# Delta rule: step sizes as logarithms in the decays' exponents, and the decay columns of all tiles from one PSUM bank

## The reference, cut to what matters

```
q = l2norm(q) * DK**-0.5;  k = l2norm(k)
beta = sigmoid(gb);  g = -exp(A_log) * softplus(ga + dt_bias)
gc = cumsum(g);  decay = exp(gc_t - gc_s)            (t >= s)
L  = beta_t * (k k^T) * decay                         (t > s);   A = L + I
u, w = A^-1 [ v * beta | k * (beta * exp(gc)) ]
v_new = u - w S;   qk = (q k^T) * decay
o = (q * exp(gc)) S + qk v_new
S_new = S * exp(g_last) + (k * exp(g_last - gc))^T v_new
```

## Time and profile before

| | |
|---|---|
| time, median of 3 runs | 945.67 us (945.03 to 946.57) |
| span of the profiled execution, first to last instruction | 943.7 us |
| the profiled execution's own time | not listed apart; the median stands 1.97 us above the span |
| PE / weight load / DVE / ACT / POOL busy | 99% / 89% / 69% / 48% / 18% |
| tile loop, 220.87 to 255.01 us | 34.14 us: PE 34.14, DVE 26.96, ACT 22.81, POOL 19.30 busy |
| elimination, 255.01 to 283.38 us | 28.37 us: PE 27.68, DVE 21.46, ACT 20.11, POOL 18.29 busy |

### The profile page before, as it was taken

The page is one execution under the profiler, slowest core; times in us unless marked ns, Lnnn a source line. Parts: engine busy times, 40 slices in busy tenths (PEclk is TensorE's granted clock), DMA queues, the critical chain, the costliest instruction groups (busy, mean ns, idle before and its releaser), DMA issues.

```text
span 943.7 us, 16891 instructions
## 1 busy us (share of the span) xinstructions
PE 931.8 (99%) x6919; PEld 841.9 (89%) x6919; DVE 648.3 (69%) x1083; ACT 452.1 (48%) x836; POOL 170.0 (18%) x198
## 2 busy tenths in 40 slices
PE   9999999999999999999999999999999999999998
PEld 7899888998889877799888999999999999888886
DVE  7627888777775565552666999999999999435321
ACT  6634454648566454554654445444444445333310
POOL 0071101103664331000002032222222220000000
PEclk9999999999999999999999999999999999999999
DMA  8624142121104084244904322222222224412221
GB/s 303 225 88 145 54 168 93 47 94 49 45 5 135 2 290 154 82 142 157 317 18 138 113 87 90 90 90 90 88 73 74 79 89 152 147 64 93 78 89 56
DMA packets 73820, 103.70 MB, mean 110 GB/s; under 512 B 2576, under 2 KB 53904, under 8 KB 73360
## 3 DMA queue, kind: packets, MB, share of 16 engines
q1 hardware_dynamic: 73744, 102.63, 32.6%
HBM read 92.27 MB, written 10.35 MB: 109 GB/s over the span
## 4 chain that ended last, share of the span: by engine, by line
PE 51%; DVE 3%; ACT 2%; POOL 1%; issue 1%; ACTq 0%; POOLq 0%; DVEq 0%
PE bank L1222 8%; PE bank L1220 8%; PE bank L1221 8%; PE bank L538 5%; PE bank L537 5%; PE bank L536 5%; PE bank L484 2%; PE bank L486 1%; PE bank L485 1%; PE bank L466 1%; PE bank L562 1%; PE bank L1034 1%; PE bank L564 1%; PE bank L563 1%; PE bank L1036 1%
## 5 line engine op out<-in xcount | busy, mean ns | idle before, releaser
L2168 DVE TENSOR_TENSOR wlo<-wraw,whi 128x2048 fp32r<-128x2048 f32 (+1 forms) x56 | 126.2, 2253 | 102.2 <-ACT whi L1617 93.0
L1617 ACT ACTIVATE whi<-wraw 128x2048 fp32r<-128x2048 f32 (+1 forms) x58 | 109.3, 1885 | 101.9 <-PE bank L538 72.8
L498 PE MATMUL bank<-hhi,whi 128*128 128x320 f32 x352 | 116.4, 331 | 0.6 <-issue 0.6
L500 PE MATMUL bank<-hhi,wlo 128*128 128x320 f32 x352 | 108.7, 309 | 0.0
L499 PE MATMUL bank<-hlo,whi 128*128 128x320 f32 x352 | 108.7, 309 | 0.0
L498 PEld LDWEIGHTS bank<-hhi,whi 128*128 128x128 f32 x352 | 66.2, 188 | 5.0 <-issue 3.6
L499 PEld LDWEIGHTS bank<-hlo,whi 128*128 128x128 f32 x352 | 66.2, 188 | 3.0 <-issue 2.4
L500 PEld LDWEIGHTS bank<-hhi,wlo 128*128 128x128 f32 x352 | 66.1, 188 | 0.0
L536 PE MATMUL bank<-whi,hhi 128*128 128x512 f32 x150 | 58.4, 389 | 0.0
L537 PE MATMUL bank<-wlo,hhi 128*128 128x512 f32 x150 | 58.4, 389 | 0.0
L538 PE MATMUL bank<-whi,hlo 128*128 128x512 f32 x150 | 58.3, 389 | 0.0
(11 more groups left out here) (491 smaller groups left out, 2690.4 us busy)
## 6 DMA issues: line engine op xcount, KB each, us to landing
wraw<-in_w_in SPq DMA_DIRECT2D x13, 1024.0 KB, 5.5
wraw<-in_w_gate SPq DMA_DIRECT2D x11, 1024.0 KB, 5.2
wraw<-in_w_up SPq DMA_DIRECT2D x11, 1024.0 KB, 5.1
wraw<-in_w_down SPq DMA_DIRECT2D x10, 1024.0 KB, 5.1
kTs<-in_cache_sb_k SPq DMA_DIRECT2D x8, 512.0 KB, 4.4
vraw<-in_cache_sb_v SPq DMA_DIRECT2D x8, 512.0 KB, 4.9
wraw<-in_w_mix_out SPq DMA_DIRECT2D x4, 1024.0 KB, 6.3
kmT<-in_cache_mem_k SPq DMA_DIRECT2D x8, 512.0 KB, 6.2
```

What stands on the lines that cost most here:

```text
L498: T.matmul(o, wh[:, k, cs], hhi[:, k, hs], start=(k == 0), stop=False)
L500: ins = T.matmul(o, wl[:, k, cs], hhi[:, k, hs], start=False, stop=(k == KD - 1))
L1617: V(wv(whi, i), wv(wraw, i), ACT.Copy).then_inc(s["w_hi_ready"], 1)
L2168: V.tensor_tensor(wv(wlo, i), wv(wraw, i), wv(whi, i).bitcast(F32), ALU.subtract)\
```

## The change

The step size enters as a logarithm. With softplus(-gb) = -log(beta), one absolute value, exponential and logarithm on 40 columns serve both gates (`gsoft`). `lnc` is the log norm of the key minus softplus(-gb) minus `vscale`, and it is subtracted from the summed g in column form, so the exponentials already hold beta and the norms' ratio; the values are scaled by `vscale` in place of `beta`. Gone are `ratio`, `beta`, POOL's `beta_source`, PE's `beta_rows`, DVE's second product on `LT` and its product on `bege`. The clamp RMAX is 60 in place of 14. The columns of all tiles are made at once, by five matmuls into one bank, in front of the first "grow". ACT takes their exponentials once, after tile 1's large ones.

```diff
-RMAX = 14.0
+RMAX = 60.0
-        rsrc = [[at(f"rsrc{n}{m}", [P, HEADS, P], CQ + TILE * (2 * n + m)) for m in range(2)] for n in range(2)]
+        rsrc = [at(f"rsrc{n}", [P, HEADS, P], CQ + TILE * n) for n in range(2)]
...
@@ block.tensor @@
+            def decay_columns():
+                b = take(("gcol", 0))
+                of_tiles = gdec[:, 0:PT, :].rearrange("p t h -> p (t h)")
+                T.matmul(gcol(b, "sum"), uptri[:, :], of_tiles, start=True, stop=True)
+                T.matmul(gcol(b, "all"), ones[:, :], of_tiles, start=True, stop=True)
+                T.matmul(gcol(b, "own"), ones[:, :], flat(gown), start=True, stop=True)
+                T.matmul(gcol(b, "sum16"), up16[:, :], gdec[:, PT, :], start=True, stop=True)
+                done(T.matmul(gcol(b, "all16"), same16[:, :], gdec[:, PT, :], start=True, stop=True), ("gcol", 0))
             def decay_rows(i):
-                b = take(("gcol", i))
-                T.matmul(bank[b][:, 0:4], (uptri if i < PT else up16)[:, :], gdec[:, i, :], start=True, stop=True)
-                if i == PT:
-                    T.matmul(bank[b][:, 8:8 + HEADS * DEC_BATCH], ones[:, :], flat(gown), start=True, stop=True)
-                done(T.matmul(bank[b][:, 4:8], (ones if i < PT else same16)[:, :], gdec[:, i, :],
-                              start=True, stop=True), ("gcol", i))
                 pe.wait_ge(s["decay_src"], i + 1)
...
-            def beta_rows(i):
-                pe.wait_ge(s["beta_src"], i + 1)
-                b = take(("brow", i))
-                done(T.matmul(bank[b][:, :], ones[:, :], flat(rsrc[i % 2][1]), start=True, stop=True), ("brow", i))
...
             pe.wait_ge(s["gates"], 1)
+            decay_columns()
             decay_rows(0)
             for i in range(NT):
...
-                beta_rows(i)
@@ block.gpsimd @@
-            def beta_source(i):
...
-                G.tensor_tensor(rsrc[i % 2][1][:, :, :], spread(ident[:, :], 1, [P, HEADS, P]),
-                                spread(ratio[:, i, :], 2, [P, HEADS, P]), ALU.mult).then_inc(s["beta_src"], 1)
@@ block.scalar @@
             for i in range(NT):
-                evacuated(e, ("gcol", i))
-                V(kdec[:, i, :], gcs[:, i, 2, :], ACT.Exp)
-                V(bege[:, i, :], gcs[:, i, 3, :], ACT.Exp)
...
                 e.wait_ge(s["dif_ready"], i + 1)
                 V(scr[4 + i % 2][:, :, :], scr[4 + i % 2][:, :, :], ACT.Exp).then_inc(s["dt_ready"], 1)
...
                 V(scr[6 + i % 2][:, :, :], quad(b), ACT.Exp).then_inc(bank_free[b], 1)
+                if i == 1:
+                    V(kdec[:, :, :], gcs[:, :, 2, :], ACT.Exp)
+                    V(bege[:, :, :], gcs[:, :, 3, :], ACT.Exp)
+                    V(etot[:, 0:PT, :], gcs[:, 0:PT, 1, :], ACT.Exp)
+                    V(etotS[:, :, :], etotS[:, :, :], ACT.Exp).then_inc(s["small_exp"], 1)
@@ block.vector @@
             def log_norms():
-                link(V.tensor_tensor(ratio[:, :, :], lnr[:, :, :, 1], lnr[:, :, :, 0], ALU.subtract))
...
+                link(V.tensor_tensor(vscale[:, :, :], lnr[:, :, :, 0], lnr[:, :, :, 1], ALU.subtract))
+                link(V.tensor_tensor(lnc[:, :, :], lnr[:, :, :, 1], gsoft[:, 1, :, 0:4], ALU.subtract))
+                V.tensor_tensor(lnc[:, :, :], lnc[:, :, :], vscale[:, :, :], ALU.subtract)\
+                    .then_inc(s["l2_ready"], 1)
...
+            def decay_columns():
+                b = filled(dve, ("gcol", 0))
+                for part, ts in (("", slice(0, PT)), ("16", slice(PT, NT))):
+                    upto, total = [gcol(b, n + part).rearrange("p (t h) -> p t h", h=HEADS) for n in ("sum", "all")]
+                    V.tensor_tensor(gcs[:, ts, 0, :], upto, lnc[:, ts, :], ALU.subtract)
+                    V.tensor_tensor(gcs[:, ts, 3, :], upto, lnr[:, ts, :, 0], ALU.add)
+                    ins = V.tensor_copy(gcs[:, ts, 1, :], total)
+                link(ins)
+                V.tensor_copy(flat(etotS), gcol(b, "own"))
+                V.tensor_tensor(gcs[:, :, 2, :], gcs[:, :, 1, :], gcs[:, :, 0, :], ALU.subtract).then_inc(bank_free[b], 1)
...
             for i in range(NT):
-                dve.wait_ge(s["small_exp"], i + 1)
-                V.tensor_tensor(bege[:, i, :], bege[:, i, :], beta[:, i, :], ALU.mult)
...
-                evacuated(dve, ("kk", i))
-                b = filled(dve, ("brow", i))
-                V.tensor_tensor(LT[i][:, :, :], LT[i][:, :, :], quad(b), ALU.mult).then_inc(bank_free[b], 1)
```

More of the change, by code:

```diff
@@ L313, in mixed, with gcol @@
             return qkvz[:, f, :] if f < 4 else yb[:, f - 4, :] if f < 6 else yc[:, f - 6, :]
+        def gcol(b, part):
+            c, n = {"sum": (0, 16), "all": (16, 16), "sum16": (32, 4), "all16": (36, 4), "own": (40, 32)}[part]
+            return bank[b][:, c:c + n]
         def at_banks(n):
@@ L790, in _ @@
             ring[0] = "gdn"
-            def decay_rows(i):
-                b = take(("gcol", i))
-                T.matmul(bank[b][:, 0:4], (uptri if i < PT else up16)[:, :], gdec[:, i, :], start=True, stop=True)
-                if i == PT:
-                    T.matmul(bank[b][:, 8:8 + HEADS * DEC_BATCH], ones[:, :], flat(gown), start=True, stop=True)
-                done(T.matmul(bank[b][:, 4:8], (ones if i < PT else same16)[:, :], gdec[:, i, :],
-                              start=True, stop=True), ("gcol", i))
+            def decay_columns():
[6 more added lines that the diff above has]
+                done(T.matmul(gcol(b, "all16"), same16[:, :], gdec[:, PT, :], start=True, stop=True), ("gcol", 0))
+            def decay_rows(i):
                 pe.wait_ge(s["decay_src"], i + 1)
                 b = take(("grow", i))
-                done(T.matmul(bank[b][:, :], ones[:, :], flat(rsrc[i % 2][0]), start=True, stop=True), ("grow", i))
+                done(T.matmul(bank[b][:, :], ones[:, :], flat(rsrc[i % 2]), start=True, stop=True), ("grow", i))
             def key_products(i):
@@ L1531, in _ @@
                 else:
-                    filled(pool, ("brow", PT))
+                    filled(pool, ("grow", PT))
                     for n in range(PT, PT + 2):
@@ L1824, in decay_source @@
                 for h in range(HEADS):
-                    V(rsrc[i % 2][0][:, h, :], tri(i)[:, :], ACT.Copy, scale=gdec[:, i, h:h + 1])
+                    V(rsrc[i % 2][:, h, :], tri(i)[:, :], ACT.Copy, scale=gdec[:, i, h:h + 1])
                 for h in range(HEADS):
@@ L1831, in _ @@
             e.wait_ge(s["gates_act"], 1)
[L1832 to L1835, removed]
+            link(V(gsoft[:, 0], gba[:, :, :], ACT.Abs))
+            link(V(gsoft[:, 0], gsoft[:, 0], ACT.Exp, scale=-1.0))
+            V(gsoft[:, 0], gsoft[:, 0], ACT.Ln, bias=ones[:, 0:1])
             V(nA[:, :], alog[:, :], ACT.Exp).then_inc(s["gates_act"], 1)
@@ L1843, in _ @@
             decay_source(0)
-            V(ratio[:, :, :], ratio[:, :, :], ACT.Exp, scale=-0.5).then_inc(s["ratio_act"], 1)
+            V(vscale[:, :, :], vscale[:, :, :], ACT.Exp)
             decay_source(1)
@@ L2339, in beta_decay @@
                 dve.wait_ge(s["gates_act"], 2)
[L2340 to L2344, removed]
+                link(V.tensor_scalar(gsoft[:, 1], gba[:, :, :], 0.0, None, ALU.max))
+                link(V.tensor_tensor(gsoft[:, 1], gsoft[:, 1], gsoft[:, 0], ALU.add))
+                link(V.scalar_tensor_tensor(out=gdec[:, :, :], in0=gsoft[:, 1, :, 4:8], scalar=-1.0,
                                             in1=spread(nA[:, :], 1, [P, NT, HEADS]), op0=ALU.mult, op1=ALU.mult))
```

45 lines of the change are left out of this document (13 added, 32 removed).

## The result

The changed kernel took 938.44 us (median of 4, 937.68 to 939.22), the kernel before 945.41 us beside it (4 runs): ratio 0.9926, 95% interval 0.9915 to 0.9938. The span fell from 943.7 to 936.6 us.

The account below looks back on a forecast made before the run. PE was taken to bound the kernel nearly everywhere, with ACT limiting the elimination's head. Savings of 3.44 + 1.00 + 0.27 = 4.71 us took the span from 943.7 to 939.0; plus 1.97, 941.0 us, range 939.2 to 943.4.

Parts of the forecast that it names:

- brow: Tile loop, PE: four 512-column matmuls on step sizes go, 0.86 us each, saving 3.44 us by the last fill's end.
- gcol: Tile loop, PE: eleven small column matmuls become five, saving 1.00 us, bounds 0.84 and 1.32.
- Is something late in the loop?: Tile loop: DVE's sum for tile 2's "grow" matmul keeps 0.6 us of slack; cost 0, bounds 0 and 0.5 us.
- Head of the elimination: Start of the elimination: ACT limits it, so of the fifth 512-column matmul's 0.86 to 1.02 us about 0.27 arrives.
- After that ... Cost 0: Later elimination steps, last level and chains over tiles: same instructions, driven by PE's progress, so cost 0.
- The offset of 1.97 us: Whole kernel: the median of the runs lies 1.97 us above the profiled span, added to the forecast span of 939.0.
- Rival 1: Elimination: all of the fifth 512-column matmul's saving arrives; gain 5.4 us, or 6.1 with PE waits vanishing; chance 0.18.
- Rival 2: Tile loop and elimination: "grow" sources 0.5 us late for three tiles, plus a 0.7 us wait; gain 2.5 us; chance 0.19.
- Rival 4: Head of the elimination: more PE waits drop the clock from 2.4 to 1.2 GHz; slower, 951 or 969 us; chance 0.04.

## Why the prediction was right where it was, and where it failed

- *"brow"*, 3.44 us: right, by the trace (4.77 less the columns) and by the four put back (3.44).
- *"gcol"*, 1.00 us: too small. Measured 4.77 - 3.44 = 1.33. I had taken a group's price from its own starts and left out the 0.08 us by which it delays what follows the row matmul: 4 x 0.44 + 0.67 - (1.03 + 0.08) = 1.32, my upper bound.
- The rule of the Trainium skill, "TensorE: Matmul & The Clock Gate", section LDWEIGHTS, had given an estimate of 1.28, nearer than my reading of the rows. The trace agrees with it: two loads of 107 ns are 0.214 us, and a small matmul was measured at 0.22.
- *"Is something late in the loop?"*, cost 0: right, with 0.4 us of slack. That DVE and POOL lose work stood in the sum as nothing, and it is no gain by itself; but it is what keeps the slack. With the old load put back, 4.9 of the 7 us were lost by the medians and 3.7 in the trace; with one of the two put back, 2.9 (DVE) or 2.6 (POOL) by the medians.
- *Head of the elimination*, 0.27 us: right in kind, 0.15 at step 5. The 0.20 over the whole elimination in the table is less than its scatter and shows nothing.
- ***"After that ... Cost 0"* is the step that failed.** It argued that the same instructions keep their distances. They did not: the number of takes moved the banks (0.67 us), and the five POOL instructions less turned the order of DVE and POOL at `tlo_gate` (the last two rows of the table, 1.27 us; 0.9 of it is the order, by the traces of two kernels in which it was forced, the rest is open). Together about 1.9 us. With 0.33 more by the columns, 0.12 ahead of the stage and 0.07 less at the elimination, the 4.7 become 7.0. The turn of the order could not be read from the rows shown, and that it went the right way was luck; the move of the banks could have been counted.
- *The offset of 1.97 us* from span to median was too large: every run here lies about 1.7 to 1.8 us above its own span. With 1.76, as in the profiled run of the changed kernel, the forecast would have been 940.8 us.
- *Rival 1* had a gain nearer the measured one, 5.4 to 6.1 us, but by waits within the elimination; those did not go. *Rival 2*'s place, the source of tile 2, was the right one: it is where DVE's load put back makes PE wait 1.30 us. *Rival 4*'s mechanism does not happen in the changed kernel's elimination (clock 1.00 in its window), and does in two variants.

## What to carry to other kernels

When an edit changes how often a ring of buffers is taken, follow the ring to the next stage: which buffer it meets there, and how late that one is freed. Where two engines with a shared path start within some tenths of a microsecond of each other, look at the order as at a coin that any edit upstream can turn, and fix it by a wait if one side is on the path. And before leaving out the relief of a second engine because the first is busy 99%, subtract: find how long that engine's result lies ready before the first one needs it, and whether the result would still be in time with the old load.

## What the runs showed of the hardware that I had not expected

- *POOL starts later with five products more, some 300 us behind them.* At the first of POOL's sums, PE's release being the same, six traces of kernels with the five POOL products (the one before, its variants and those with the product put back) have it 13.43 to 13.45 us ahead of a fixed PE matmul, and eight traces of kernels without them 13.74 or 13.75. Behind its releaser it starts after 0.45 to 0.47 us in the six and after 0.16 in the eight. At this place, before and after:

```profile
541.45 9.01 DVE L2703 TENSOR_TENSOR slo<-sraw,shi 128x1280 fp32r<-128x1280 f32 x4
...
541.47 2.61 POOL L1585 TENSOR_TENSOR traw_up<-wraw 128x512 f32<-128x512 f32 x1 [25.23 <-PE bank L486]
```
```profile
535.45 1.30 POOL L1576 TENSOR_TENSOR traw_up<-wraw 128x512 f32<-128x512 f32 x1 [24.94 <-PE bank L490]
...
535.71 7.40 DVE L2690 TENSOR_TENSOR slo<-sraw,shi 128x1280 fp32r<-128x1280 f32 x3
```

  0.30 us sooner, POOL is ahead of DVE's low part in place of behind it; ACT's rounding and DVE's next parts follow, and at tlo_gate DVE is then first. The kernel with only POOL's products put back differs from the changed one in nothing else, and is in the first group. Why it starts 0.30 us sooner is open: I did not vary POOL's program by other instructions.
- *The clock after a wait.* With both loads back and the order forced, PE waited 1.66 us for DVE at the head of the elimination, and right behind the wait the granted clock fell to 0.50 for about 3 us (windows; busy times, clock behind them):

```profile
255.00:257.00 2.00, 0.66 (x25) 0.69 (x29) 1.97 (x5) 1.05 (x3) 2.00 (x3) 0.85 0.00 0
257.00:259.00 2.00, 2.00 (x25) 1.84 (x17) 0.89 (x3) 1.29 (x4) 1.92 (x4) 0.50 0.00 0
```

  In the kernel with both loads and no forced order a wait of 1.64 us there left the clock at 1.00 in the profiled run (942.52 us, the fastest of ten). From the first matmul behind the wait (step 3) to step 4 it is 2.95 us with the lower clock and 1.70 without. So behind a wait of this length the clock sometimes falls, at a cost of 1.25 us here. The Trainium skill, "TensorE: Matmul & The Clock Gate", section "HAM oscillation", speaks of longer gaps than this 1.66 us; here the measurement decides.
- *The elimination scatters.* From the last fill's end to the elimination's end the same instructions of PE took 30.62 to 31.27 us in three traces of the kernel before and its variants, and 29.91 to 30.94 in four of the changed kernel and its variants with the elimination as it is. PE stops inside a step with nothing that the profile shows as the cause ("issue", 0.5 us in step 5 of the changed kernel's trace, none in step 5 of the three others, which have such stops elsewhere). This is open. It may also be why medians of these kernels differ by some tenths without another reason.
